# Nine broadcast norm rows loaded one at a time behind freed weight slots, on one core

## The chip, the core and the metric

The kernel runs on one core of a Trainium2 chip. The metric is the device time of one execution in microseconds (us), the median of several runs. The engines named here are TensorE (PE; its weight loads are listed as PEld), VectorE (DVE), ScalarE (ACT), GpSimd (POOL) and SyncE (SP), which only issues transfers. Transfers from the chip's memory (HBM) to on-chip memory are issued by SyncE, ScalarE or GpSimd and carried out by the core's 16 DMA engines.

## What is computed

Two models one behind the other, all in float32, on one sequence of 256 tokens of width 1024: two layers of a first block, then two hybrid attention layers. The part that this change touches is the first:

```python
def rmsnorm(x, g, eps=NORM_EPS):
    xf = x.astype(jnp.float32)
    y = xf * lax.rsqrt(jnp.mean(xf * xf, -1, keepdims=True) + eps)
    return (y * g.astype(jnp.float32)).astype(x.dtype)

def swiglu(x, w_gate, w_up, w_down):
    return (jax.nn.silu(x @ w_gate) * (x @ w_up)) @ w_down

...
    for layer in range(DEPTH):
        ng = norm_gains[layer]
        hdn = swiglu(rmsnorm(x, ng[0]), ffn1_w_gate[layer], ffn1_w_up[layer], ffn1_w_down[layer])
        x = x + 0.5 * rmsnorm(hdn, ng[1])
        hdn = rmsnorm(x, ng[2])
        hdn = nsa_ssd_mixer(hdn, cos, sin, ab_w_in[i], a_cmp_pe_k[i], a_cmp_w1_k[i],
...
        x = x + rmsnorm(hdn, ng[3])
        hdn = swiglu(rmsnorm(x, ng[4]), ffn2_w_gate[layer], ffn2_w_up[layer], ffn2_w_down[layer])
        x = x + 0.5 * rmsnorm(hdn, ng[5])
```

The gains ng[1], ng[3] and ng[5] of both layers, the gain and bias of the second mixer's norm (c_ln_g, c_ln_b) and the gain of the last norm (final_g_2) are the nine rows of this change. Each multiplies or is added along the free dimension, so each is needed in all 128 partitions.

## The kernel before

**Weights.** All large weights pass through `ring`, six slots of 1 MB (128 partitions x 2048 floats). The list of blocks is fixed (`plan_weights`). SyncE loads block n as soon as the semaphore `slot_used` has reached n - 5, that is when TensorE has freed the slot of block n - 6 (`load_slot`, `load_ffn`; lines 304 and 324 issue). TensorE raises `slot_used` by one with its last use of a block.

**The first feed-forward layer** is the first of four of the same form. In the reference this is `swiglu`, with 2816 hidden columns. It takes eleven rounds q = 0 to 10, each with a gate block, an up block and a down block (33 blocks, so `slot_used` ends it at 33). The first round multiplies directly (line 516). From the second on a scheme with sums of weight quarters is used, so that fewer products are needed: VectorE forms the sums of the next round's gate and up block (`weight_sums`, lines 601 to 609), TensorE multiplies (`first_half`, then the down products of the round before at line 555, then `second_half`; the products of both halves are issued at line 502), VectorE and ScalarE put the results together (lines 591, 593, 627 to 640) and VectorE writes the hidden block (line 643, `hid`), which TensorE multiplies with the down block in the next round. TensorE frees the down block in the middle of a round and the gate and up block in the half behind it.

The first half of a round begins with one product of the gate block itself and then one of the up block itself; the sums come behind them. A product is four matmuls over the contraction, and each matmul is recorded as two instructions, so it stands in the timeline as x8.

**Small parameters.** `first_loads` (ScalarE's queue) fetches what is needed at once. `later_loads` (GpSimd's queue, line 682 issues) fetches 26 further parameters: nine rows of 1024 floats broadcast to 128 partitions (`everywhere`; 512 KB written each), eight lambda rows of 64 floats and three rows of 16 broadcast in the same way, and six small arrays. GpSimd waits once, until `slot_used` is 6, and then issues all 26 without another wait; all of them raise one semaphore, `later_in`. TensorE, ScalarE and VectorE each wait for all 26 at the end of the first feed-forward layer (lines 2360, 2389, 2416), before the first of these rows is read (line 410). GpSimd's own next work comes behind that, in the first mixer.

```python
2347            nc.gpsimd.memset(hT[:, :, META - 1:META], 0.0).then_inc(h_zero, 1)
2348            pool.wait_ge(slot_used, NSLOT)
2349            later_loads(nc.gpsimd)
```

Of the kernel before, what the change touches and what calls it, by code (L numbers as in the profile page):

```python
# [30 lines left out]
NSLOT = 6  # L31
# [153 lines left out]
def model_kernel(nc, d, out, stop=None):  # L185
    ctx = ExitStack()
    with ctx:
        def sb(name, shape):
            return ctx.enter_context(nc.sbuf_tensor(name, shape, F32))

        def sem(name):
            return ctx.enter_context(nc.semaphore(name))
# [6 lines left out]
        gains = sb("gains", [P, 12, D])  # L199
# [15 lines left out]
        LN_G, LN_B, FINAL_G, LAMB = 6, 7, 8, 9  # L215
# [11 lines left out]
        slot_used = sem("slot_used")  # L227
# [425 lines left out]
        def everywhere(v):  # L653
            return v.rearrange("(o n) -> o n", o=1).broadcast_to([P, v.shape[0]])
# [24 lines left out]
        def later_loads(eng):  # L679

            def load(dst, src):
                eng.dma_start(dst, src).then_inc(later_in, 16)
                n_later()

            for i, (l, g) in enumerate((l, g) for l in range(2) for g in (1, 3, 5)):
                load(gains[:, i, :], everywhere(d["norm_gains"][l, g]))
            load(gains[:, LN_G, :], everywhere(d["c_ln_g"][0]))
            load(gains[:, LN_B, :], everywhere(d["c_ln_b"][0]))
            load(gains[:, FINAL_G, :], everywhere(d["final_g_2"]))
            for l in range(2):  # L690
                for i, n in enumerate(("lam_q1_2", "lam_k1_2", "lam_q2_2", "lam_k2_2")):
                    c = (4 * l + i) * 64
                    load(gains[:, LAMB, c:c + 64], everywhere(d[n][l]))
            load(dt_bias, everywhere(d["b_dt_bias"][0]))
            load(a_log, everywhere(d["b_a_log"][0]))
            load(d_skip, everywhere(d["b_d_skip"][0]))
            for l in range(2):
                load(forget[:, l:l + 1], d["b_forget_2"][l].rearrange("(p o) -> p o", o=1))
            load(w2k[:, 0:64], d["a_cmp_w2_k"][0])
            load(w2k[:, 64:128], d["a_cmp_w2_k"][0])  # L700
            load(w2v, d["a_cmp_w2_v"][0])
            load(xm[:, :], d["meta_tokens_2"])

        row_in, row_t, col_in, rows_t = sem("row_in"), sem("row_t"), sem("col_in"), sem("rows_t")

# [1639 lines left out]
        @block.gpsimd  # L2345
        def _(pool):
            nc.gpsimd.memset(hT[:, :, META - 1:META], 0.0).then_inc(h_zero, 1)
            pool.wait_ge(slot_used, NSLOT)
            later_loads(nc.gpsimd)
# [119 lines left out]
```

## Time and profile before

| | |
|---|---|
| median of 3 runs | 1898.8 us (1897.58 to 1910.72) |
| the profiled execution, first to last instruction | 1893.8 us |
| chain that ended last, by engine | PE 89%, DVE 5%, ACT 2%, issue 2%, DMA 1% |
| mean granted clock of TensorE | 0.967 of full |
| bytes moved, mean rate | 232.74 MB, 123 GB/s |
| of these GpSimd's queue (q0, software_dynamic) | 5.12 MB in 1840 packets |
| of these SyncE's queue (q1, hardware_dynamic) | 224.97 MB in 191584 packets |
| first feed-forward layer, TensorE products | 17.7 to 241.7 us |

A timeline has one row for a run of equal instructions: its start, how long the run lasts, the engine, the line, the operation, what it writes and reads, how many there are (x8), and in brackets the idle time ahead of it with what ended it. A stretch of the span is given from the span's start. The granted clock is that of TensorE, as a share of its full 2.4 GHz.

### The profile page before, as it was taken

The numbers are of one execution on the slowest core, as the hardware profiler recorded it, in microseconds if no ns is written. First come the engines' busy times: TensorE is split into PE (matmuls) and PEld (weight loads), VectorE is DVE, ScalarE is ACT, GpSimd is POOL, SyncE is SP. The second block draws the span as 40 slices with busy tenths as digits, with TensorE's granted clock in tenths as the row PEclk, the third lists the DMA queues.
The fourth block names the chain that finished last, engine by engine and source line by source line (L and its number), as shares of the span: only waits on it lengthen the run. The fifth ranks groups of instructions, "written<-read, shape, count | busy, mean of one in ns | idle before, by whom it ended". The sixth has DMA issues, their size and how long they took to land.

```text
span 1893.8 us, 25538 instructions
## 1 busy us (share of the span) xinstructions
PE 1788.9 (94%) x10478; PEld 1358.7 (72%) x10478; DVE 843.5 (45%) x1790; ACT 413.6 (22%) x1010; POOL 57.5 (3%) x71
## 2 busy tenths in 40 slices
PE   7999989999999999999988999899998999999997
PEld 5777768776587876878766778587886677556774
DVE  3244333744334335444357747434433444324353
ACT  1000022533200002000146412200002253113521
POOL 0200000000000000000003130000000000000000
PEclk9999998999999999999998959999998999999999
DMA  6754554212344544544433300254556762467520
GB/s 225 251 181 142 137 134 134 67 67 81 120 156 136 198 134 134 177 157 161 158 103 105 126 24 1 90 162 150 168 157 102 114 96 84 88 82 106 99 89 22
DMA packets 194168, 232.74 MB, mean 123 GB/s; under 512 B 27028, under 2 KB 175960, under 8 KB 194056
## 3 DMA queue, kind: packets, MB, share of 16 engines
q1 hardware_dynamic: 191584, 224.97, 43.3%
q0 software_dynamic: 1840, 5.12, 0.9%
q8 instruction: 84, 1.38, 0.3%
q10 hardware_dynamic: 632, 1.04, 0.1%
q14 instruction: 28, 0.23, 0.0%
HBM read 230.07 MB, written 1.05 MB: 122 GB/s over the span
## 4 chain that ended last, share of the span: by engine, by line
PE 89%; DVE 5%; ACT 2%; issue 2%; DMA 1%; ACTq 0%; DVEq 0%
PE ps L502 26%; PE ps L275 25%; PE ps L555 15%; PE ps L462 6%; PE ps L516 3%; PE ps L1629 1%; DMA ring<-in_ffn_w_up 1%; PE ps L1464 1%; PE ps L358 1%; PE ps L2148 1%; PE ps L2164 1%; PE ps L2152 1%; PE ps L2178 1%; PE ps L2183 1%; PE ps L1646 1%
## 5 line engine op out<-in xcount | busy, mean ns | idle before, releaser
L275 PE MATMUL ps<-hT,ring 128*128 128x272 f32 (+2 forms) x1504 | 363.9, 396 | 3.6 <-issue 1.3
L275 PEld LDWEIGHTS ps<-hT,ring 128*128 128x128 f32 (+1 forms) x1504 | 280.8, 190 | 65.2 <-issue 8.5
L555 PE MATMUL ps<-ring,arena 128*128 128x512 f32 x704 | 309.4, 592 | 0.0
L555 PEld LDWEIGHTS ps<-ring,arena 128*128 128x128 f32 x704 | 130.4, 190 | 147.3 <-issue 147.3
L502 PE MATMUL ps<-arena 128*128 128x128 f32 x1920 | 222.7, 276 | 0.0
L502 PEld LDWEIGHTS ps<-arena 128*128 128x128 f32 x1920 | 219.4, 193 | 0.0
L502 PEld LDWEIGHTS ps<-hT,ring 128*128 128x128 f32 x1280 | 156.8, 193 | 26.0 <-issue 19.1
L502 PE MATMUL ps<-hT,ring 128*128 128x128 f32 x1280 | 163.6, 276 | 6.4 <-DMA ring<-in_ffn_w_up 6.4
L627 DVE TENSOR_TENSOR arena<-arena,ps 128x256 f32<-128x256 f32 x40 | 16.8, 421 | 256.5 <-ACT arena L591 256.5
L640 DVE TENSOR_TENSOR arena<-arena,ps 128x384 f32<-128x384 f32 x80 | 44.2, 554 | 183.4 <-PE ps L502 183.4
L593 ACT ACTIVATE arena<-arena 128x512 f32<-128x512 f32 x40 | 25.2, 630 | 384.7 <-DVE arena L640 384.7
L591 ACT ACTIVATE arena<-ps 128x512 f32<-128x512 f32 x40 | 23.9, 597 | 356.4 <-PE ps L502 356.4
L462 PE MATMUL ps<-ring,arena 128*128 128x512 f32 (+1 forms) x192 | 86.8, 607 | 4.2 <-DVE more L1253 3.5
L502 PE MATMUL ps<-hT,arena 128*128 128x128 f32 x640 | 84.5, 275 | 0.0
L502 PE MATMUL ps<-arena,ring 128*128 128x128 f32 x640 | 84.5, 275 | 0.0
L502 PEld LDWEIGHTS ps<-hT,arena 128*128 128x128 f32 x640 | 77.9, 192 | 0.0
L502 PEld LDWEIGHTS ps<-arena,ring 128*128 128x128 f32 x640 | 77.9, 192 | 0.0
L462 PEld LDWEIGHTS ps<-ring,arena 128*128 128x128 f32 (+1 forms) x192 | 32.8, 178 | 56.6 <-issue 51.4
L2282 DVE TENSOR_TENSOR arena<-ps,cst 128x288 f32<-128x288 f32 (+2 forms) x40 | 20.3, 507 | 115.9 <-PE ps L2152 65.8
L358 PE MATMUL ps<-cst,arena 128*128 128x128 f32 x128 | 27.4, 398 | 37.7 <-DVE arena L438 37.7
L601 DVE TENSOR_TENSOR arena<-ring 128x512 f32<-128x512 f32 x80 | 51.6, 683 | 19.7 <-DMA ring<-in_ffn_w_up 11.6
L516 PE MATMUL ps<-hT,ring 128*128 128x256 f32 x256 | 57.1, 384 | 0.0
(408 smaller groups left out, 2165.7 us busy)
## 6 DMA issues: line engine op xcount, KB each, us to landing
ring<-in_ffn_w_gate SPq DMA_DIRECT2D x44, 1024.0 KB, 5.5
ring<-in_ffn_w_up SPq DMA_DIRECT2D x44, 1024.0 KB, 5.8
ring<-in_ffn_w_down SPq DMA_DIRECT2D x44, 1024.0 KB, 5.0
ring<-in_w_in SPq DMA_DIRECT2D x32, 1024.0 KB, 9.4
ring<-in_ab_w_in SPq DMA_DIRECT2D x12, 1024.0 KB, 5.3
ring<-in_w_out SPq DMA_DIRECT2D x8, 1024.0 KB, 5.0
ring<-in_ab_w_out SPq DMA_DIRECT2D x6, 1024.0 KB, 4.9
ring<-in_c_w_k SPq DMA_DIRECT2D x4, 1024.0 KB, 5.5
```

The lines of the kernel that those rows point to most:

```text
L275: last = nc.tensor.matmul(o, l, r, start=(i == 0), stop=(i == len(pairs) - 1))
L358: m = nc.tensor.transpose(o, xn[:, t, k * P:(k + 1) * P], ident)
L462: m = nc.tensor.matmul(o[:, h, :], lhs(k, t), slot2(n)[:, k % 2, h * 512:(h + 1) * 512], start=(k == 0), stop=(k == nk - 1))
L502: m = nc.tensor.matmul(o, left[:, k, :], right[:, k, :], start=(k == 0), stop=(k == 3))
L516: m = nc.tensor.matmul(ps[:, 6 + w, 256 * i:256 * (i + 1)], slot8(s0 + w)[:, k, i * P:(i + 1) * P], hT[:, k, META:], start=(k == 0), stop= ...
L555: m = nc.tensor.matmul(ps[:, 2 * t + h, :], hid[:, q % 2, i, t * P:(t + 1) * P], slot2(s0 + 3 * q + 2)[:, i, h * 512:(h + 1) * 512], start ...
L591: nc.scalar.activation(gu_e[:, :, 1:6:4], gu_a[:, :, 0:2], ACT.Copy).then_inc(a_copied, 1)
L593: nc.scalar.activation(gate_s.rearrange("p (i n) -> p i n", i=4), gu_e[:, 0, 1:5], ACT.Silu).then_inc(silu_done, 1)
L601: nc.vector.tensor_tensor(d_q[:, w, 0], w_part(n + w, 1, 0), w_part(n + w, 1, 1), ALU.add).then_inc(w_sums, 1)
L640: nc.vector.tensor_tensor(gu_e[:, w, 1:4], gu_e[:, w, 1:4], gu_b[:, w, 0:3], ALU.add).then_inc(b_taken, 1)
L1464: m = nc.tensor.matmul(bank_a(n)[:, 0:S], slot8(s)[:, c, (j % 2) * P:(j % 2 + 1) * P], MB[0][:, c, :], start=(c == 0), stop=(c == KD - 1))
L2282: dlink(dve, nc.vector.tensor_tensor(pr, ps[0:r, 0:2, 0:w], msk.rearrange("p (o n) -> p o n", o=1).broadcast_to([r, 2, w]), ALU.add))
```

## The change

`later_loads` issues the 17 other parameters first, in the order that they had, and then the nine rows in the order that they had. In front of each row GpSimd now waits for `slot_used`: for 8 at the first, 10 at the second, and so on by twos to 24 at the ninth. The wait for 6 ahead of the whole function stays. What is loaded, and where to, is the same, and the engines that wait for `later_in` still wait for 26 transfers.

```diff
-            for i, (l, g) in enumerate((l, g) for l in range(2) for g in (1, 3, 5)):
-                load(gains[:, i, :], everywhere(d["norm_gains"][l, g]))
-            load(gains[:, LN_G, :], everywhere(d["c_ln_g"][0]))
-            load(gains[:, LN_B, :], everywhere(d["c_ln_b"][0]))
-            load(gains[:, FINAL_G, :], everywhere(d["final_g_2"]))
             for l in range(2):
                 for i, n in enumerate(("lam_q1_2", "lam_k1_2", "lam_q2_2", "lam_k2_2")):
                     c = (4 * l + i) * 64
...
             load(w2v, d["a_cmp_w2_v"][0])
             load(xm[:, :], d["meta_tokens_2"])
+            rows_later = [(i, d["norm_gains"][l, g]) for i, (l, g) in enumerate((l, g) for l in range(2) for g in (1, 3, 5))]
+            rows_later += [(LN_G, d["c_ln_g"][0]), (LN_B, d["c_ln_b"][0]), (FINAL_G, d["final_g_2"])]
+            for n, (i, row) in enumerate(rows_later):
+                eng.wait_ge(slot_used, NSLOT + 2 * n + 2)
+                load(gains[:, i, :], everywhere(row))
```

On GpSimd, at the start of its program, the order of instructions changes as follows (- before, + after; `gains` is the tensor that holds the rows, `in_...` the input read, and the numbers are partitions x elements):

```order
 L2347 MEMSET hT 128x8
-L682 DMA gains<-in_norm_gains 128x1024 x6
-L682 DMA gains<-in_c_ln_g 128x1024
-L682 DMA gains<-in_c_ln_b 128x1024
-L682 DMA gains<-in_final_g 128x1024
 L682 DMA gains<-in_lam_q_2 128x64
 L682 DMA gains<-in_lam_k_2 128x64
```

The nine rows no longer stand ahead of the lambda rows and of the small arrays behind these. The second place is the end of the same list of loads, just ahead of GpSimd's first work in the mixer (line 1351); here the order is shown with what each instruction waits for:

```order
 L682 DMA small<-in_a_cmp_w_v 64x64
 L682 DMA xm<-in_meta_tokens 16x1024
+L682 DMA gains<-in_norm_gains 128x1024 [waits slot_used] x6
+L682 DMA gains<-in_c_ln_g 128x1024 [waits slot_used]
+L682 DMA gains<-in_c_ln_b 128x1024 [waits slot_used]
+L682 DMA gains<-in_final_g 128x1024 [waits slot_used]
 L2376 UNCONDITIONAL_BRANCH
 L1351 MEMSET arena 128x4x3 [waits hidden]
```

The nine rows stand there now, each behind a wait of its own. The order on TensorE, VectorE, ScalarE and SyncE is the same as before.

## Rows read from the trace of the kernel before

**Rows 1.** The page: busy time, share of the span and instructions of each engine.

```profile
PE 1788.9 (94%) x10478; PEld 1358.7 (72%) x10478; DVE 843.5 (45%) x1790; ACT 413.6 (22%) x1010; POOL 57.5 (3%) x71
```

**Rows 2.** Waits of PE, 0 to 240 us: engine, line, releaser, us, times, longest.

```profile
PE ps L502 <- DMA ring<-in_ffn_w_up: 6.4, 1, 6.4
```

**Rows 3.** Timeline of SP, 26 to 230 us.

```profile
32.03 0.38 SPq L324 DMA_DIRECT2D ring<-in_ffn_w_up  x1
...
65.36 0.37 SPq L324 DMA_DIRECT2D ring<-in_ffn_w_down  x1
...
70.78 0.37 SPq L324 DMA_DIRECT2D ring<-in_ffn_w_up  x1
84.72 0.37 SPq L324 DMA_DIRECT2D ring<-in_ffn_w_down  x1
87.61 0.37 SPq L324 DMA_DIRECT2D ring<-in_ffn_w_gate  x1
...
113.41 0.37 SPq L324 DMA_DIRECT2D ring<-in_ffn_w_down  x1
...
118.84 0.37 SPq L324 DMA_DIRECT2D ring<-in_ffn_w_up  x1
...
210.13 0.37 SPq L304 DMA_DIRECT2D ring<-in_ffn_w_down  x1
```

**Rows 4.** Timeline of PE within 60 to 125 us.

```profile
72.15 5.52 PE L502 MATMUL ps<-arena 128*128 128x128 f32 x48
...
89.74 1.06 PE L502 MATMUL ps<-hT,ring 128*128 128x128 f32 x8
...
97.24 2.08 PE L502 MATMUL ps<-hT,ring 128*128 128x128 f32 x8 [6.45 <-DMA ring<-in_ffn_w_up]
...
99.11 7.25 PE L502 MATMUL ps<-arena 128*128 128x128 f32 x48
```

**Rows 5.** DMA issues, 104 to 215 us: size, median us from issue to landing.

```profile
ring<-in_ffn_w_up SPq DMA_DIRECT2D x5, 1024.0 KB, 6.8
```

**Rows 6.** Timeline of POOL, 64 to 80 us.

```profile
65.48 3.33 POOL L682 DMA_DIRECT2D gains<-in_norm_gains  x6 [64.62 <-PE ps L555]
...
70.36 0.55 POOL L682 DMA_DIRECT2D gains<-in_lam_q  x1
...
78.74 0.53 POOL L682 DMA_DIRECT2D xm<-in_meta_tokens  x1
```

**Rows 7.** DMA queues, 65 to 86 us: packets, MB, share of 16 engines.

```profile
q0 software_dynamic: 1336, 4.73, 62.0%
q1 hardware_dynamic: 1343, 2.14, 31.8%
```

**Rows 8.** Windows: stretch, us, PE busy (x), PEclk, DMA share, GB/s.

```profile
94.00:96.00 2.00, 0.00 (x0) 0.98 0.92 314
...
100.00:102.00 2.00, 2.00 (x11) 0.50 0.73 253
```

**Rows 9.** Timeline of SP, 520 to 700 us, second feed-forward layer.

```profile
522.25 0.38 SPq L324 DMA_DIRECT2D ring<-in_ffn_w_up  x1
...
691.02 0.37 SPq L304 DMA_DIRECT2D ring<-in_ffn_w_down  x1
```

**Rows 10.** DMA queues, 86 to 97 us.

```profile
q0 software_dynamic: 504, 0.39, 35.0%
```

**Rows 11.** Timeline of DVE, 44 to 90 and 112 to 130 us.

```profile
67.95 0.55 DVE L640 TENSOR_TENSOR arena<-arena,ps 128x384 f32<-128x384 f32 x1 [2.51 <-PE ps L502]
...
71.23 0.69 DVE L643 TENSOR_TENSOR arena<-arena 128x512 f32<-128x512 f32 x1
...
127.99 1.28 DVE L601 TENSOR_TENSOR arena<-ring 128x512 f32<-128x512 f32 x2
```

**Rows 12.** Timeline of DVE, 195 to 245 us.

```profile
238.40 0.69 DVE L410 TENSOR_TENSOR arena<-ps,gains 128x512 f32<-128x512 f32 x1 [5.62 <-PE ps L555]
```

**Rows 13.** Windows, all engines: busy (x), PEclk, DMA share, GB/s.

```profile
1080.00:1120.00 40.00, 37.30 (x498) 26.97 (x496) 23.42 (x36) 9.42 (x12) 3.29 (x2) 0.61 0.09 28
```

## The prediction

> **What bounds the kernel now.** I began with the page's busy times: TensorE has work in 94% of the span [rows 1], VectorE and ScalarE far less. So only what makes TensorE wait, or slows its clock, is worth time. The change touches only transfers that GpSimd issues in the first feed-forward layer, so I read that layer next, with the waits of TensorE in the first 240 us. One of them is for a weight transfer: line 502 waits 6.4 us, once, for a block of the up matrix [rows 2]. The timelines say which block. SyncE issues it at 70.78 us [rows 3]; TensorE finishes the eight products with the gate block (89.74 + 1.06 = 90.80 us), and its next product, the first that reads the up block, starts only at 97.24 us, released by that transfer [rows 4]. So it took some 26.4 us from issue to use, where an undisturbed up load lands 6.8 us after its issue [rows 5].
>
> What lies in its way is seen in the GpSimd timeline: from 65.48 us on it issues the nine rows back to back, 4.7 MB, and then the 17 small loads until 78.74 + 0.53 = 79.27 us [rows 6]. Between 65 and 86 us GpSimd's queue (q0) moved 4.73 MB in 1336 packets and SyncE's (q1) only 2.14 MB in 1343 [rows 7].
>
> The stall has a second part. TensorE's granted clock is 0.98 of full in 94 to 96 us, so it was at its upper level (2.4 GHz) until about then, when the engine had stood still for 4 to 5 us, and 0.50 (1.2 GHz) in 100 to 102 us, when it worked again [rows 8]. The eight products at 97.24 us take 2.08 us where the same shape takes 1.06, the 48 behind them 7.25 where 48 take 5.52 at 72.15 us [rows 4].
>
> **What the stall costs, three ways.** (a) Its pieces: 6.45 wait + (2.08 - 1.06) + (7.25 - 5.52) = 9.20 us. (b) The period of the loop, from one down load's issue to the next: 84.72 - 65.36 = 19.36 us just before, although the whole burst is issued in it, and 113.41 - 84.72 = 28.69 us with the stall [rows 3]; 9.33 us more. (c) The same layer without such loads: from the issue of its second up load behind a wait to that of its last down load, the first layer takes 210.13 - 32.03 = 178.10 us [rows 3], the second feed-forward layer 691.02 - 522.25 = 168.77 us [rows 9]; 9.33 us. (b) and (c) agree to the hundredth, so the first layer loses nothing to these loads except this one stall. That is the most the change can take away there: **9.3 us**.
>
> **The change part by part.** No engine's computing instruction is added, removed or moved, and SyncE's queue is the same row for row; GpSimd issues the same 26 loads in another order, with nine waits among them. Its waits cost no computing engine anything: GpSimd's next work stands far behind in the mixer.
>
> *The 17 small loads* go first, at the same wait (six freed slots, 65.5 us). Their issue takes 79.27 - 70.36 = 8.9 us [rows 6], so they are out at about 74.4 us. What they cost the DMA engines is not seen alone. Below: in 86 to 97 us, behind the rows, q0 took 35.0% of 11 us = 3.9 us of the 16 engines for 504 packets [rows 10]. Above: all of q0's 1336 + 504 = 1840 packets less 9 x 128 = 1152 of the rows are 688, at the same price 5.3 us.
>
> *A row* moves 512 KB. All of q0's share in 65 to 86 us was 62.0% of 21 us = 13.0 us [rows 7], over nine rows at most 1.45 us each. That is an average in a flood; from below it is nothing.
>
> *The up load that stalled* is now issued at 70.78 us beside the small loads and one row, whose wait (eight freed slots) is met at that same 70.78 us, so it goes out right after the small ones, at 74.4 us. Lands: 70.78 + 6.8 = 77.6 us with nothing in its way, 77.6 + 5.3 + 1.45 = 84.3 us with everything charged to it. TensorE needs it at 90.8 us: 6.5 us are left in the worst sum, and the 9.3 us go whole. VectorE wants these blocks earlier for its sums (lines 601 to 609): in an undisturbed period it starts at 127.99 us on blocks of which the up load was issued at 118.84 [rows 3, 11], 9.15 us later, so here it starts at about 79.9 us and may wait up to 84.3 - 79.9 = 4.4 us. Behind that it has a gap of 2.51 us before its next work, the line 640 that waits for TensorE [rows 11]; the rest (4.4 - 2.5 = 1.9 us) moves the hidden block (line 643), which is ready at 71.23 + 0.69 = 71.92 us [rows 11] for products that stand behind the 48 that end at 77.67 us [rows 4]. That is 5.7 us early, so 1.9 us late reaches nobody.
>
> *The other eight rows* go out at 10, 12, ... 24 freed slots. SyncE's loads wait for the same counts, so each leaves beside one weight load: the second at 87.61 us beside a gate block; the fourth at 118.84 - 9.33 = 109.5 us beside an up block; the last beside a down block, four rounds of 19.36 us after the down load at 113.41 - 9.33 = 104.1 us, so at 181.5 us [rows 3]. From the second on the pattern is gate, down, up. A row beside an up load lets it land 6.8 + 1.45 = 8.3 us after issue, before VectorE's 9.15 us. So nothing is added: 0 us each. If that cover were gone, TensorE's would remain: 20.0 - 6.8 = 13.2 us, with 20.0 = 90.80 - 70.78.
>
> A rule is to be weighed here. The packets of the two queues in 65 to 86 us are equal in number (1336 and 1343) and not in bytes [rows 7]. The Trainium skill, "DMA: Bandwidth & Descriptors", section "Queues, rings and completion order", says why: each DMA engine takes turns between its queues packet by packet. The trace agrees. By it a row (4 KB packets) overtakes a gate or up load (about 1 KB packets) even when issued behind it; by order of arrival a row issued together with or after the weight load would cost it nearly nothing. The sum would be the same 9.3 us by either, with 8.3 or 6.8 us to landing.
>
> *The wait at the layer's end.* PE, ACT and DVE wait for all 26 loads before the normalisation. VectorE's first instruction behind that wait, line 410, runs at 238.40 us [rows 12], so 229.1 us in the new time; the last row leaves at 181.5 us, 47.6 us earlier. Nothing is added.
>
> *Sum.* -9.3 + 0 + 0. The profiled span is 1893.8 us, so its successor's is 1884.5; the profiled run stands 5.0 us below the median of the runs shown (1898.8), and I take the difference over: 1898.8 - 9.3 = **1889.5 us**, 0.5% less.
>
> After the layer everything moves forward rigidly, since its loads wait for freed slots, not for time. One thing doesn't move quite rigidly: in later stages the clock falls in short waits (mean 0.61 in 1080 to 1120 us, that is 15.6 us of full clock lost there [rows 13]), and where a fall begins may come out a little otherwise when all is shifted. The nearest priced fall is the one above, 1.0 + 1.7 = 2.7 us; I take 0 and keep one fall to either side for the range.
>
> **The rivals.**
> *A small stall stays.* For it: q0's small packets are dear, 3.9 us for 0.39 MB [rows 10], and now go out in the same 9 us in which the gate and up loads are issued. Against it: 6.5 us of margin. If the up load landed 2.2 us late (93.0 us), TensorE would wait 2.2 us at full clock, since the clock held for some 4 us of standing still [rows 4, 8]: net -7.1, 1891.7 us. It begins where the small loads and a row cost over 13.2 us together, twice my upper sum.
> *The change doesn't do what it says.* The small loads, not the rows, held the queue, or the wait that is removed is taken up by another: 1898.8 us. Against it: rows are 92% of q0's bytes, and (c) shows the layer without such loads at 9.33 us less, with no other wait appearing.
> *Slower: the stall comes back at each up load with a row beside it.* The fourth and the seventh row leave together with an up load. If a row held that load for over 13.2 us, TensorE would stand still twice, at the price seen once: 2 x 9.3 - 9.3 = +9.3, 1908.1 us. Against it: 1.45 us a row, nine times too little. The Trainium skill, same page, section "Anatomy of one DMA", fits 2.0 us plus the bytes over 436 GB/s to a GpSimd-issued load; that would be an estimate of 3.2 us for a row, above my 1.45, and no row here shows one alone. By it too the up load lands in time for TensorE (10.0 of 20.0 us), but VectorE would wait about 0.9 us in those periods, which its gap of 2.5 us takes.
>
> **How the numbers follow.** Forecast (stall gone whole) 82%; a small stall 7%; no gain 4%; slower by returning stalls 3%; more gained than 9.3, by clock falls that come out better, 4%. The likeliest's own range: one fall of 2.7 us to either side, 1886.8 to 1892.2. The three runs shown spread from 1897.58 to 1910.72, their lower two within 1.2 us; I widen by about 2 below, and above to the small stall and half of the way to no gain: **1884.5 to 1896.5 us**. About 1% (19 us) is what a measurement of this kernel can tell from no change; no case reaches it by its own price, so faster by over 1% has 2%, within 1% 96%, slower by over 1% 2%.
>
> **What the changed profile would show.** GpSimd: 17 small loads from 65.5 to about 74.4 us, then rows at about 74.4, 87.6, 104.1, 109.5, 126.4, 142.8, 148.3, 165.1 and 181.5 us. The down loads' issues at 84.72 and then 104.1 us, 19.36 us apart. TensorE's wait for the up load gone from the list of waits, its clock at 1.00 from 85 to 105 us. VectorE's wait at line 601 at about 80 us: 0 to 4.4 us instead of 7.2 and 9.3. Line 410 at 229.1 us. The prediction fails if line 502 still waits for a transfer in the first layer, if a row's landing takes over 13 us, or if a later stage differs by more than one clock fall.

## The result and the profile after

| | before | after |
|---|---|---|
| median | 1898.34 us (11 runs, 1896.37 to 1920.43) | 1886.91 us (11 runs, 1879.41 to 1888.26) |
| ratio after to before | | 0.9926, 95% interval 0.9903 to 0.9949 |
| profiled execution | 1893.8 us | 1884.1 us |
| mean granted clock, profiled execution | 0.967 | 0.969 |

The change gains 11.4 us by the medians. The ratio says 0.74%, 14.1 us of 1898.8, and its interval reaches from 9.7 to 18.4 us. The forecast of 9.3 us lies below all of it, by a little; as a time the ratio gives 1898.34 x 0.9926 = 1884.3 us, just under the lower end of the stated range (1884.5). The ratio goes with the means, and three times that stand apart weigh in it, 1910.72 and 1920.43 us before and 1879.41 us after: without them the means are 1897.8 and 1886.8 us, 11.0 us apart. The two profiled executions differ by 9.7 us, nearly as forecast. So the mechanism has to be checked in the trace, and then why an ordinary execution gains more than this pair of traces.

GpSimd's timeline after, as [rows 6] of before:

```profile
65.42 0.73 POOL L682 DMA_DIRECT2D gains<-in_lam_q  x1 [64.56 <-PE ps L555]
...
74.03 0.53 POOL L682 DMA_DIRECT2D xm<-in_meta_tokens  x1
74.53 0.59 POOL L682 DMA_DIRECT2D gains<-in_norm_gains  x1
87.69 0.54 POOL L682 DMA_DIRECT2D gains<-in_norm_gains  x1 [12.57 <-PE ps L502]
104.15 0.53 POOL L682 DMA_DIRECT2D gains<-in_norm_gains  x1 [15.93 <-PE ps L555]
...
181.65 0.53 POOL L682 DMA_DIRECT2D gains<-in_final_g  x1 [15.94 <-PE ps L555]
```

The 17 small loads go out from 65.42 to 74.56 us, the first row at 74.53, and the others at the freed slots, each within 0.3 us of the time that the prediction worked out. SyncE's timeline after, beside [rows 3]:

```profile
31.97 0.38 SPq L324 DMA_DIRECT2D ring<-in_ffn_w_up  x1
...
65.30 0.37 SPq L324 DMA_DIRECT2D ring<-in_ffn_w_down  x1
...
70.72 0.37 SPq L324 DMA_DIRECT2D ring<-in_ffn_w_up  x1
84.66 0.37 SPq L324 DMA_DIRECT2D ring<-in_ffn_w_down  x1
...
104.04 0.37 SPq L324 DMA_DIRECT2D ring<-in_ffn_w_down  x1
...
200.75 0.37 SPq L304 DMA_DIRECT2D ring<-in_ffn_w_down  x1
```

The down loads are 84.66 - 65.30 = 19.36 and 104.04 - 84.66 = 19.38 us apart, where before the second distance was 28.69. From the first up load behind a wait (31.97 us) to the last down load it is 168.78 us, where the second feed-forward layer took 168.77 [rows 9]. TensorE's timeline in the place of [rows 4]:

```profile
89.68 1.95 PE L502 MATMUL ps<-hT,ring 128*128 128x128 f32 x16
91.46 5.52 PE L502 MATMUL ps<-arena 128*128 128x128 f32 x48
96.82 7.03 PE L555 MATMUL ps<-ring,arena 128*128 128x512 f32 x16
```

The products with the gate and the up block stand in one group of 16 again, the 48 behind them take 5.52 us, so both the wait and the slow clock are gone. The window from 85 to 105 us agrees: TensorE busy all of it, granted clock 1.00 (the third number from the end).

```profile
85.00:105.00 20.00, 20.00 (x136) 16.17 (x135) 12.34 (x22) 1.23 (x2) 1.07 (x2) 1.00 0.57 198
```

VectorE, as [rows 11], shows what wasn't forecast:

```profile
83.14 0.69 DVE L601 TENSOR_TENSOR arena<-ring 128x512 f32<-128x512 f32 x1 [3.19 <-DMA ring<-in_ffn_w_gate]
87.41 0.69 DVE L601 TENSOR_TENSOR arena<-ring 128x512 f32<-128x512 f32 x1 [3.58 <-DMA ring<-in_ffn_w_up]
...
92.88 0.69 DVE L643 TENSOR_TENSOR arena<-arena 128x512 f32<-128x512 f32 x1 [0.23 <-ACT arena L593]
```

Its sums wait for the gate block until 83.14 us and for the up block until 87.41 us, 3.19 + 3.58 = 6.8 us where 0 to 4.4 was forecast. The up block, issued at 70.72 us, took 16.7 us to land, where the prediction had 84.3 us as the worst sum:

```profile
ring<-in_ffn_w_up SPq DMA_DIRECT2D x1, 1024.0 KB, 16.7
```

TensorE wants the block at about 90.7 us, and the hidden block (line 643, ready at 93.57 us) at 96.82 us, so nobody waited for it; but of the margin of 6.5 us that the prediction kept, 3.3 us were left. Behind the stall the layer shows nothing but the shift: line 410 runs at 229.03 us, forecast 229.1, and from there to the end it is 1655.1 us where it was 1655.4.

```profile
229.03 0.69 DVE L410 TENSOR_TENSOR arena<-ps,gains 128x512 f32<-128x512 f32 x1 [5.62 <-PE ps L555]
```

### The profile page after: what moved, and what is told of

Its sections match the earlier page's. It is cut to its first block, busy times and chain, and to the rows that moved or that the text cites. A ratio compares the mean times of both kernels' runs of the same rounds, so it can differ in the third digit from the quotient of the medians.

```text
span 1884.1 us, 25538 instructions
## 1 busy us (share of the span) xinstructions
PE 1786.0 (95%) x10478; PEld 1355.7 (72%) x10478; DVE 843.9 (45%) x1790; ACT 413.7 (22%) x1010; POOL 57.7 (3%) x71
## 4 chain that ended last, share of the span: by engine, by line
PE 91%; DVE 5%; ACT 2%; issue 2%; ACTq 0%; DVEq 0%
PE ps L502 27%; PE ps L275 26%; PE ps L555 16%; PE ps L462 6%; PE ps L516 3%; PE ps L1629 1%; PE ps L1464 1%; PE ps L358 1%; PE ps L2148 1%; PE ps L2164 1%; PE ps L2152 1%; PE ps L2178 1%; PE ps L2183 1%; PE ps L1646 1%; DVE x L418 0%
```

## The experiments

**Why the gain is larger than 9.3 us: the same two kernels again.** The kernel before was run and traced again, several times (e1) and once each in e5 and e6, and so was the changed one, several times (e2). Neither has an edit.

> The kernel before, once more, for its own trace and the spread of its times. In question is why the measured gain (medians 1898.34 to 1886.91 us, 11.4 us) is larger than the 9.3 us that the stall costs in the profiled execution of before. Theory A (the stall differs from execution to execution, and the profiled one has a small one): the trace shows the wait of line 502 for the up block again, longer than 6.45 us where the span is longer than 1893.8 us by the same amount, and everything outside 85 to 105 us as long as before; times around 1898, spread over several us. Theory B (the stall is fixed at 9.3 us, and the rest is clock falls in later stages): the wait is 6.4 to 6.6 us and a difference in span lies behind 240 us.

> The changed kernel, once more. Theory A: times within 3 us of each other around 1886.5, since what varied is gone; no wait of TensorE for a weight block in the first layer; the difference to the kernel before run beside it is 9 to 13 us. Theory B: as large a spread as before's, difference near 9.3 us.

> The kernel before, for one more trace. The two traces so far have a stall of 28.69 - 19.36 = 9.33 and 29.18 - 19.37 = 9.81 us, and span 1893.8 and 1895.0 us, both low among the times of before (median 1898.4 us, 1894.5 to 1900.3 in the bulk); the times of the changed kernel lie within 3 us in the bulk. Theory A (the stall varies): the stall here is another one again, between 8 and 14 us. Theory B (it is fixed): 9.3 to 9.8 us.

> As the look before: a further value of the stall, theory A 8 to 14 us, theory B 9.3 to 9.8 us.

Measured: e1 1898.43 us (12 runs), its ratio to the kernel before beside it 1.0017 (0.9989 to 1.0045); e2 1886.99 us against 1898.46 us, ratio 0.9953 (0.9927 to 0.9980), which is 11.5 us by the medians and 8.9 by the ratio; e5 1900.75 and e6 1899.36 us, one run each. The traces, cut in three at the first down load behind a wait and at line 410, the stall being what the period from 84 us has over 19.37:

| trace | span | to the first down load | stall | from line 410 to the end |
|---|---|---|---|---|
| before, the one of the prediction | 1893.8 | 45.98 | 9.33 | 1655.4 |
| e1 before | 1895.0 | 44.36 | 9.81 | 1657.7 |
| e6 before | 1897.6 | 45.77 | 10.88 | 1657.9 |
| e5 before | 1899.0 | 46.51 | 11.38 | 1658.0 |
| after | 1884.1 | 45.92 | 0 | 1655.1 |
| e2 after | 1885.3 | 44.88 | 0 | 1657.3 |

The waits of TensorE in the first layer, e5 (the longest stall):

```profile
PE ps L502 <- DMA ring<-in_ffn_w_up: 9.2, 1, 9.2
```

and its period, by SyncE's timeline:

```profile
85.25 0.37 SPq L324 DMA_DIRECT2D ring<-in_ffn_w_down  x1
...
90.68 8.98 SPq L324 DMA_DIRECT2D ring<-in_ffn_w_up  x1
116.00 0.37 SPq L324 DMA_DIRECT2D ring<-in_ffn_w_down  x1
```

What theory A said of the stall holds: it is another one in each execution, 9.3 to 11.4 us, and the trace from which I predicted has the smallest of the four. That everything else stays as long does not hold, and there theory B has a share: in e1 the stall is only 0.5 us longer, and 2.3 us of the longer span lie behind line 410. TensorE waited 6.45, 7.89, 8.85 and 9.22 us in the order of the table. The load that GpSimd issues last before the change (`xm`) took 17.3, 18.7, 19.9 and 20.1 us to land, in the same order, so a longer stall goes with slower small loads; what made them slower wasn't found. The part behind line 410 takes one of two lengths in both kernels, about 1655.3 or 1657.7 us. The difference lies in its first 42 us, by the granted clock in windows that begin at line 410, first before, then e1:

```profile
238.40:280.00 41.60, 35.31 (x153) 0.96 0.59 142
```

```profile
237.27:278.87 41.60, 35.36 (x139) 0.88 0.55 132
```

Over the six traces without a stall that the runs here gave (after, e2, e4, e8, e10, e11; spans 1884.1, 1885.3, 1886.0, 1884.5, 1886.1, 1884.8, mean 1885.1) and the four of before (mean 1896.4) the difference is 11.2 us. (The traced execution of e7, 1877.4 us, is left out: its clock behind the layer was higher, 0.974 in the mean; one of the eleven times of the changed kernel, 1879.41 us, is of that kind too.) Of the 11.2 us, 10.35 is the mean stall, 0.8 comes because three of four but only three of six have the longer rest, 0.1 the time ahead. The sum is near the 11.4 us between the medians. The 0.8 us hang on which of two rests ten traces happened to have, so that share isn't shown to be lasting. Times of e1 spread from 1896.73 to 1901.15 in the bulk, those of e2 beside it from 1885.06 to 1888.44; a part of what varied is gone with the stall.

**The two halves of the change apart.** e3 has the new order without the nine waits, e4 the waits with the rows still ahead of the small loads.

```diff
             for n, (i, row) in enumerate(rows_later):
-                eng.wait_ge(slot_used, NSLOT + 2 * n + 2)
                 load(gains[:, i, :], everywhere(row))
```

> The 17 small loads first, then the nine rows without their waits, so the burst of rows stays and only begins at 74.5 us instead of 65.5 us. Theory 1 (the rows' bytes in one burst hold up the weight block; packets take turns): the up block issued at 70.7 us, which landed at 87.4 us with one row beside it, has eight more rows of up to 1.45 us each in its way, so it lands at up to 99 us, and TensorE waits for it from 90.8 us, 4 to 8 us; the period from 84.7 us stays 5 to 11 us too long; the time is that of before within 3 us. Rival (the small loads behind the rows were what held the queue, the order is enough): no wait of TensorE, down load at 104.0 us, 1887 us.

e3: 1893.82 us against 1898.46, ratio 0.9977 (0.9963 to 0.9992). The up block landed 24.4 us after its issue, TensorE waited 4.4 us, and the period was 110.77 - 84.52 = 26.25 us:

```profile
PE ps L502 <- DMA ring<-in_ffn_w_up: 4.4, 1, 4.4
```

```profile
84.52 0.37 SPq L324 DMA_DIRECT2D ring<-in_ffn_w_down  x1
...
110.77 0.37 SPq L324 DMA_DIRECT2D ring<-in_ffn_w_down  x1
```

The stall (6.88 us) stays, as theory 1 said, and the rival falls. The time was not within 3 us of before, as I had it, but 4.6 us below. The burst begins 9 us later and may reach the block with fewer rows still ahead; that reading wasn't tested.

For e4 the block of code with the rows and their waits stands ahead of the lambda loads again:

```diff
+            for n, (i, row) in enumerate(rows_later):
+                eng.wait_ge(slot_used, NSLOT + 2 * n + 2)
+                load(gains[:, i, :], everywhere(row))
             for l in range(2):
                 for i, n in enumerate(("lam_q1_2", "lam_k1_2", "lam_q2_2", "lam_k2_2")):
...
             load(xm[:, :], d["meta_tokens_2"])
-            for n, (i, row) in enumerate(rows_later):
-                eng.wait_ge(slot_used, NSLOT + 2 * n + 2)
-                load(gains[:, i, :], everywhere(row))
```

> The nine rows first, each behind its wait (8, 10, ... 24 freed slots), and the 17 small loads behind the last row, at about 181.7 to 190.6 us. Theory 1: no wait of TensorE, time 1887 us as with the whole change; the up block issued at 70.7 us now has one row and no small load beside it and lands at about 79 us instead of 87.4, so VectorE's line 601 waits for nothing at 80 us. The small loads now lie beside the gate and up block of 184.3 and 187.0 us, which VectorE wants at about 196 us: it may wait there by up to 7 us, TensorE by nothing (it wants them at 206). Rival (the small loads must go early): a wait of TensorE at about 206 us or at the layer's end, 229 us.

e4: 1887.7 us, ratio 0.9925 (0.9898 to 0.9952), no wait of TensorE for a weight block. With one row and no small load beside it the up block landed after 8.0 us:

```profile
ring<-in_ffn_w_up SPq DMA_DIRECT2D x1, 1024.0 KB, 8.0
```

At the other end the small loads now meet the gate block of the last round: VectorE waits 2.35 us for it (line 601 at 197.62 us) and 4.50 us for the up block (202.81 us), which landed after 16.7 us; TensorE doesn't wait at all. So the waits alone do what the whole change does; the new order is neither needed nor harmful.

**What in the burst made the stall: rows or small loads.** e7 keeps the burst of nine rows at 65 us and puts only the small loads behind 12 freed slots; e8 issues the small loads with no row beside them (the rows at 12, 13, ... 20).

```diff
             load(gains[:, FINAL_G, :], everywhere(d["final_g_2"]))
+            eng.wait_ge(slot_used, 12)
             for l in range(2):
```

> The order of before, the nine rows in one burst at 65.5 us, but the 17 small loads wait for 12 freed slots (about 104 us). It tells what of the stall is the rows' and what the small loads'. Theory 1 (as in the prediction: the rows' 13.0 us are what counts): the up block lands at 70.8 + 6.8 + 13.0 = 90.6 us, just when TensorE wants it, and the small loads had added the rest: wait 0 to 1 us, time 1888 us. Theory 2 (packets take turns and a row's packet of 4 KB goes for each of 1 KB, so the rows cost the block more than their own transfer): wait 3 us or more, time 1891 to 1896 us. Theory 3 (the small loads alone make the stall): no wait and the up block lands before 84 us.

e7: 1886.57 us, ratio 0.9925 (0.9900 to 0.9949): the whole gain, with the burst of rows in place. The queues in 62 to 83 us, and VectorE and TensorE where it was close:

```profile
q0 software_dynamic: 1078, 3.96, 50.7%
q1 hardware_dynamic: 1079, 1.88, 28.4%
...
ring<-in_ffn_w_up SPq DMA_DIRECT2D x1, 1024.0 KB, 19.6
```

```profile
87.35 0.69 DVE L601 TENSOR_TENSOR arena<-ring 128x512 f32<-128x512 f32 x1 [7.45 <-DMA ring<-in_ffn_w_gate]
90.30 0.69 DVE L601 TENSOR_TENSOR arena<-ring 128x512 f32<-128x512 f32 x1 [2.26 <-DMA ring<-in_ffn_w_up]
...
95.77 0.69 DVE L643 TENSOR_TENSOR arena<-arena 128x512 f32<-128x512 f32 x1 [0.23 <-ACT arena L593]
```

```profile
89.63 1.95 PE L502 MATMUL ps<-hT,ring 128*128 128x128 f32 x16
...
96.78 0.59 PE L555 MATMUL ps<-ring,arena 128*128 128x512 f32 x1
```

Theory 1 holds to the number: the block lands at 90.3 us, expected 90.6, and nine rows cost it 19.6 - 6.8 = 12.8 us, 1.42 each. The two queues moved 1078 and 1079 packets. TensorE took the block without a wait and the hidden block 0.3 us after it was ready (95.77 + 0.69 = 96.46 us for products at 96.78). Its ten times, 1879.22 to 1888.0 us, show no stall in the others either. The rows alone bring the kernel to the edge of a stall, and what pushes it over are the small loads.

```diff
-                eng.wait_ge(slot_used, NSLOT + 2 * n + 2)
+                eng.wait_ge(slot_used, 12 + n)
```

> The 17 small loads at 65.5 us with no row beside them; the nine rows at 12, 13, ... 20 freed slots, from 104 us on. It measures the price of the small loads by themselves. With one row beside them (the changed kernel) the up block landed 16.7 and 16.2 us after its issue, with one row and no small load (the waits alone) 8.0 us, undisturbed 6.8 us. Theory 1 (small loads are dear by packet, not by byte): landing 14 to 16 us after issue, so 7 to 9 us are theirs, and while they run the DMA engines are over 90% busy at less than a fifth of the full rate. The prediction's bound was 5.3 us, landing by 12.1 us. No wait of TensorE in the first layer in either case; a row each at 104.0, 106.9 and 109.5 us doesn't make VectorE wait by more than 3 us. Time about 1887 us.

e8: 1886.33 us (one run).

```profile
q1 hardware_dynamic: 2098, 2.89, 41.0%
...
ring<-in_ffn_w_up SPq DMA_DIRECT2D x1, 1024.0 KB, 14.8
```

The 17 small loads alone, with no row beside them, delay the up block by 14.8 - 6.8 = 8.0 us. They move 0.40 MB. In 71 to 73 us GpSimd's queue had 20 packets that took the whole of the engines' time, and SyncE's queue none, although a gate and an up block were under way on it:

```profile
DMA packets 20, 0.03 MB, mean 16 GB/s; under 512 B 4, under 2 KB 4, under 8 KB 20
...
q0 software_dynamic: 20, 0.03, 104.4%
```

The same stretch is in e7, behind its small loads from 104.11 us on and long after the rows had landed: in 109 to 112 us SyncE's queue moved no packet, and the up block issued at 109.42 us landed after 15.8 us, again without a wait of TensorE.

```profile
DMA packets 33, 0.05 MB, mean 16 GB/s; under 512 B 16, under 2 KB 16, under 8 KB 32
...
q0 software_dynamic: 32, 0.03, 71.4%
```

**How much burst it takes, and what a short wait costs.** e9 lets the first five rows go together; by the edit the other four wait for 12, 14, 16 and 18 freed slots, not for 10 to 16 as the expectation says, and so stand clear of this stall (the first at 110.00 us).

```diff
-                eng.wait_ge(slot_used, NSLOT + 2 * n + 2)
+                eng.wait_ge(slot_used, 8 if n < 5 else 10 + 2 * n - 8)
```

> As the changed kernel, but the first five rows go out together (8 freed slots, 74.5 us), the other four at 10, 12, 14 and 16. The up block issued at 70.7 us landed 16.7 and 16.2 us later with one row, 24.4 us later with nine (no waits), so a further row costs it about 1.0 us, at most 1.45. Theory 1 (rows and small loads add up against the 20.0 us that TensorE gives it): lands 20.5 to 22 us after its issue, TensorE waits 0.5 to 2.4 us. On the clock: the prediction took a wait of 2.2 us to be free of a clock fall; then the period from 84.6 us is longer by the wait alone, 0.5 to 2.4 us, and the time 1888 to 1890. Rival (a wait of any length brings the clock down): the period is 2 us longer than the wait says.

e9: 1893.2 us against 1898.75, ratio 0.9959 (0.9933 to 0.9985). The up block landed after 22.9 us, outside the expected 20.5 to 22. TensorE's timeline, then its windows (the granted clock is the third number from the end):

```profile
89.40 1.06 PE L502 MATMUL ps<-hT,ring 128*128 128x128 f32 x8
93.38 2.08 PE L502 MATMUL ps<-hT,ring 128*128 128x128 f32 x8 [2.92 <-DMA ring<-in_ffn_w_up]
95.25 7.58 PE L502 MATMUL ps<-arena 128*128 128x128 f32 x48
```

```profile
90.00:92.00 2.00, 0.46 (x5) 1.00 1.03 374
92.00:94.00 2.00, 0.62 (x3) 0.68 0.98 331
94.00:96.00 2.00, 2.00 (x11) 0.50 1.07 368
```

The wait is 2.92 us, but the period is 109.88 - 84.38 = 25.50 us, 6.13 more than 19.37. The clock fell in this wait too, 0.68 in 92 to 94 us and 0.50 behind it, and cost 3.2 us on top. So the rival holds for this wait. The prediction priced a wait of 2.2 us at full clock, because the clock had held for some 4 us of standing still; that, too, came from one execution. By windows of 1 us the clock fell 5.1 us after TensorE stopped in that trace, 4.6, 3.0 and 2.3 us after in e1, e5 and e6, 2.2 us in e3 and 2.3 us here. No run has a wait of 2.2 us or less.

**Which small loads are dear.** e10 puts the eight lambda rows last, e11 the other nine small loads.

```diff
-            for l in range(2):
-                for i, n in enumerate(("lam_q1_2", "lam_k1_2", "lam_q2_2", "lam_k2_2")):
-                    c = (4 * l + i) * 64
-                    load(gains[:, LAMB, c:c + 64], everywhere(d[n][l]))
...
                 load(gains[:, i, :], everywhere(row))
+            for l in range(2):
+                for i, n in enumerate(("lam_q1_2", "lam_k1_2", "lam_q2_2", "lam_k2_2")):
+                    c = (4 * l + i) * 64
+                    load(gains[:, LAMB, c:c + 64], everywhere(d[n][l]))
```

> As the changed kernel, but the eight lambda rows (64 floats broadcast to 128 partitions) go last, behind the ninth row. Of the 17 small loads nine are left at 65.5 us. All 17 made the up block land 8.0 us later than undisturbed (14.8 against 6.8 us). Theory 1 (the lambda rows are the dear ones, 8 x 128 destinations that all read the same 256 bytes): the up block lands by 10 to 11 us after its issue (one row is beside it), and the stretch in which the DMA engines are busy at under 50 GB/s is gone from 70 to 74 us. Rival (the price is per load, by issue, about 0.5 us each): it lands at 12 to 13 us. No wait of TensorE; time 1887 us.

> The complement: only the eight lambda rows at 65.5 us, the other nine small loads behind the ninth row. Theory 1 (the lambda rows are dear): the stretch with busy DMA engines at under 50 GB/s stays, the up block lands 12 to 14 us after its issue. Rival (price per load): 11 to 12 us, and no such stretch. No wait of TensorE; time 1887 us.

e10: 1887.95 us, up block after 12.1 us. e11: 1886.6 us, after 14.4 us. One run each, no wait of TensorE for a weight block in either. Less one row (8.0 - 6.8 = 1.2 us) the nine others cost 12.1 - 8.0 = 4.1 us and the lambda rows 14.4 - 8.0 = 6.4 us. These add up to 10.5, not 8.0, so it seems that some 2.5 us are paid once, whichever kind is there; with one run each that is a reading and not shown. The dead stretch is in both. In e11 SyncE's queue moved nothing in 71 to 73 us. In e10, without a lambda row, in 69 to 71 us:

```profile
DMA packets 84, 0.07 MB, mean 37 GB/s; under 512 B 36, under 2 KB 70, under 8 KB 84
...
q0 software_dynamic: 54, 0.02, 108.4%
```

So neither theory holds as I put it. The lambda rows cost more than the others, 0.8 against 0.46 us a load, but the stretch in which the engines are busy with almost no bytes doesn't hang on them. It begins some 4 to 5 us after the first small load in e8, e10 and e11. It doesn't hang on the place of the rows either: e7 has it in 109 to 112 us (above), and e4, where all nine rows go first and the small loads from 181.25 us on, in 187 to 190 us (46 packets, 4 of them SyncE's). Only where the small loads stand directly behind the burst of nine rows, in the kernel before, is it not seen: in 86 to 89 us SyncE's queue still moved 272 packets. What causes it wasn't found.

## Why the prediction came out as it did

**The bound** was read rightly: the one wait of line 502 was what the change takes away, and the whole of it goes. With the stall out, the first layer takes 168.78 us and the second had 168.77.

**The size is the step that failed.** "The stall costs ... three ways" gives 9.20 to 9.33 us, and all three ways come from one execution. The sum was then carried to the median with "the profiled run stands 5.0 us below the median ... and I take the difference over". That difference was treated as a constant, and it wasn't. By the runs after, 1.8 us of it lie around every span (1885.9 us for a span of 1884.1). The rest is that this execution had the smallest stall of the four traced (9.33 against 9.81, 10.88 and 11.38) and the shorter of two rests. The mean stall, 10.35 us, and the rests account for 11.2 of the 11.4 us by which the medians differ. Of a stall that differs from execution to execution the prediction had no term: its case for a larger gain (4%) named only clock falls in later stages. The median after, 1886.91 us, lies at the lower end of the likeliest range (1886.8 to 1892.2), but the ratio's interval doesn't contain 9.3 us. What the ratio has beyond the medians (14.1 against 11.4 us) comes with the times that stand apart; in e2 they lie on the other side, 1911.26 and 1901.82 us with the changed kernel, and the ratio gave 8.9 us where the medians gave 11.5.

**Small loads**: bounded at 3.9 to 5.3 us from their share of the DMA engines behind the rows, 8.0 us by e8. The share of the engines in a stretch where the queues take turns didn't show that, away from the burst of rows, they keep SyncE's queue from moving at all for 2 to 3 us. The worst sum for the landing, 84.3 us, became 87.4; the margin to 90.7 us held, the one step where the error might have cost the result.

**A row**: at most 1.45 us forecast; 1.2 by e4, 1.42 by e7. For an up block with a row beside it 8.3 us from issue to landing was forecast. The medians in 86 to 206 us of the changed kernel, 8.0 and 8.4 us, mix blocks with and without a row:

```profile
ring<-in_ffn_w_gate SPq DMA_DIRECT2D x6, 1024.0 KB, 8.0
ring<-in_ffn_w_up SPq DMA_DIRECT2D x6, 1024.0 KB, 8.4
```

The two up blocks that a row was issued beside, at 109.47 and 148.21 us, took 9.6 and 9.8 us (e4: 9.5 and 9.3), and those without one 7.7 to 8.9 us, where none took over 7.0 undisturbed. The forecast charged one row, but the row issued 5 us earlier beside the down load had landed only after 6.5 and 6.7 us, beside the gate and up block; with two rows charged it would be 1.4 to 1.5 us each. The landing comes behind the 9.15 us at which VectorE starts, but VectorE reads the gate block first and didn't wait. "0 us each" came out right.

**The rule on packets** was weighed rightly. In e7 the numbers of packets again agree to one while the bytes are two to one (3.96 and 1.88 MB). That each DMA engine takes turns between its queues packet by packet is what the Trainium skill, "DMA: Bandwidth & Descriptors", section "Queues, rings and completion order", states, and the trace agrees. The fit of the Trainium skill, same page, section "Anatomy of one DMA", 2.0 us plus the bytes over 436 GB/s (estimate 3.2 us for a row), is not what a row costs its neighbour, 1.42 us by e7, nor what a row itself took beside weight blocks, 6.4 to 7.6 us from the second row of the changed kernel on.

**The rivals.** "A small stall stays" had the right suspect, the small packets, but too little weight on them, and perhaps too low a price: e9 shows a wait of 2.92 us costing 6.1. "The change doesn't do what it says" is half true in a way I hadn't seen: with the small loads moved alone (e7) the rows could have stayed. Rows 12.8 us and small loads 8.0 us each fit in the 13.2 us that TensorE leaves; together they don't. "The stall comes back" didn't happen.

## What to carry to other kernels

A transfer that lands late is an account of everything queued with it: price each item by its own measured delay, compare the sum with the time from issue to need, and ask which single item is enough to move. Take the price of a stall from several executions, above all if the times of the kernel spread; the one that the profiler caught may be the mildest. And a spread of transfers needs only as much spreading as brings the sum under the margin: nine rows in one burst were free here, in the traced execution by 0.3 us.

## What the runs showed of the hardware that was not expected

A wait of TensorE of 2.92 us was enough for the granted clock to go from 1.00 to 0.50, and the work behind it lost 3.2 us; a wait of 9.2 us (e5) cost 11.38 - 9.2 = 2.2 us beside itself. Over the six traces with a stall (waits of 2.92, 4.45, 6.45, 7.89, 8.85 and 9.22 us) the loss beside the wait was 3.2, 2.4, 2.9, 1.9, 2.0 and 2.2 us: it doesn't grow with the wait, so the shortest stalls were the dearest for their length. With the small loads of GpSimd away from the burst of rows (e8), 20 packets filled all 16 DMA engines for 2 us and no packet of the other queue moved; the same stretch is in e4, e7, e10 and e11; 17 loads of 0.40 MB in sum delayed a 1 MB load by 8.0 us, as much as five to six rows of 512 KB (1.42 us each). And one stretch behind the layer (from line 410 on) has a clock of 0.96 or 0.88 in different executions of the same kernel, worth some 2.4 us, which no change made here decides.
